# Down products of a mixture's experts in three passes of split operands, and transposes of the powers one piece earlier

## The chip, the cores and the metric

One core of one Trainium2 chip runs the whole kernel. The metric is the device time of one execution in microseconds (us), as the median of several runs; lower is better.

## What is computed

One decoder layer over 512 tokens of width 1024, in float32. First a token mixer (two recurrent branches, gates, an output projection, layer norm), then a mixture of 64 experts with top-8 routing, one shared expert and a gated embedding, and a second layer norm. The change lies in the experts, and for a small part at the very start. Of the reference:

```python
def routed_moe(x, ...):
    ...
    y = jnp.einsum('tf,fd->td', jax.nn.silu(xt @ ws_gate) * (xt @ ws_up), ws_down)
    for c in range(N_EXPERTS // EXPERT_CHUNK):
        sl = slice(c * EXPERT_CHUNK, (c + 1) * EXPERT_CHUNK)
        g = jnp.einsum('td,edf->tef', xt, w_gate[sl])
        u = jnp.einsum('td,edf->tef', xt, w_up[sl])
        hdn = jax.nn.silu(g) * u * combine[:, sl, None]
        y = y + jnp.einsum('tef,efd->td', hdn, w_down[sl])
```

Each expert has a gate and an up matrix of 1024x256 and a down matrix of 256x1024, 1 MB each. `combine` holds the routing weights, zero for all but eight experts of a token, so an expert sees 64 tokens on average (512 times 8 over 64); the kernel gathers them into 96 slots (`SL`). At the start, the mixer's input projection for the S5 branch is computed by `u_proj`, and the powers of the S5 transition are made on VectorE and turned by TensorE.

## The kernel before

The kernel is written engine by engine: one block each for SyncE (all large loads and stores), GpSimd, TensorE, ScalarE and VectorE. The order on each engine is the order of its block, and engines meet only in semaphores (`S["..."]`), each an ever growing count.

**Split operands.** A product of two float32 operands is made in one of two ways. A plain `mm` takes float32 operands as they are. `mm3` takes each operand as a high part (type fp32r, made by a ScalarE copy) and a low part (operand minus high part, made by a subtraction on VectorE or GpSimd), and adds three products: high by high, high by low, low by high (the profile's lines L701, L702, L703). Before, the experts' gate and up products are `mm3` products, and the down products (L1059) are plain.

**The experts' stage**, from about 840 us on, is a pipeline over 64 experts. Weights go through four buffers (`gate_up0..3`, `down0..3`), high parts of gate and up through two. For expert e (written `4 i + u` in the loops), one period of each engine is:

- TensorE (`expert`, from L1070 on): gate and up products of e (`gate_up`, 8 blocks of 3 products of 512 columns), eight transposes of the tokens of e+1 (`x_turn`), down products of e-1 (`down`, 2 halves by 2 blocks), two transposes of the hidden values of e (`hid_turn`).
- ScalarE: `gate_up_high(e+1)` (four copies of 128x1024), the silu of e, `rows_high(e+1)` (two copies, 128x384), `y_kept(e-1)` (first half of the down products' result from the bank to `yb`).
- VectorE: `gate_up_low(e+1)` (four subtractions of 128x1024, L1335), the product of silu, up value and routing weight (L1341), `rows_low(e+1)`, `y_kept(e-1)` (second half, L1834), and the copy of the turned hidden values from the bank, 128x192 (L1848).
- GpSimd: `gather(e+4)` (index copy L636, indirect DMA of token rows L639), then `add_expert(e-1)`: it waits for both halves of `y_kept(e-1)` and for the landing of the addition before (`rows_added`), copies an index column (L648), and issues the indirect DMA that adds up to 96 rows to `acc_dram` (L651). Additions are never in flight two at a time. `yb` has two buffers, so `y_kept(e)` waits for the landing of the addition of e-2.
- SyncE: `load_in(e+4)` once the gate and up products of e are done, `load_down(e+4)` once the down products of e are done.

Each engine's queue is in order: an instruction behind a waiting one waits too.

**The start.** `u_proj(0)` to `u_proj(7)` are eight pieces of the S5 projection (16 matmul records each, L735). Between the sixth, `u_proj(5)`, and the seventh, TensorE waits for `powers_ready` (VectorE has made the powers) and turns the powers (21 transposes, L708). VectorE waits for these (`powers_put`), copies them (L1456), works through a chain of element-wise instructions, and then makes the low parts of the transposed input (`x_low`), on which the first split products, `x_proj(0, 0)`, wait. `x_proj` also waits until ScalarE has copied all eight pieces of the projection (`u_kept`).

## Time and profile before

| | |
|---|---|
| median of 3 runs | 1528.13 us (1526.51 to 1529.31) |
| the profiled execution | 1527.41 us, span 1525.6 us |
| mean granted TensorE clock | 0.964 of full speed |
| TensorE busy | 92% of the span |
| HBM read, written | 297.35 MB, 34.65 MB |

The span runs from the first to the last instruction of the profiled execution; some 2 us of its time lie outside. A row of the timeline gives start and duration of an instruction, or of a run of equal ones (`x4`), and in brackets how long the engine had been idle before and what released it. DVE is VectorE, ACT ScalarE, POOL GpSimd, PE TensorE, SP SyncE. The durations of neighbours overlap a little, so for the rate at which instructions follow one another the starts are what counts.

### The profile page before, as it was taken

The page shows a single profiled execution, that of the slowest core. Times are in us where ns is not written, and L with a number is a line of the kernel's source. Part 1 is how long each engine was busy: PE and PEld are TensorE (multiplying, and loading weights), DVE is VectorE, ACT ScalarE, POOL GpSimd, SP SyncE. Part 2 cuts the span into 40 slices and gives each one's busy share as a digit, 9 for nine tenths or more (in the row PEclk, how much of TensorE's full clock was granted, in tenths as well). Part 3 has the DMA queues.
Part 4 walks back from the last instruction along what each step waited for, and adds up shares of the span by engine and source line. Part 5 has one row for each costly group of instructions (what it writes and reads, how often), then busy time and mean ns, then how long its engine had stood idle before and what let it go on. Part 6 is the DMA issues. An engine that isn't in the chain of part 4 may idle for free.

```text
span 1525.6 us, 18528 instructions
## 1 busy us (share of the span) xinstructions
PE 1408.9 (92%) x6293; PEld 931.9 (61%) x6293; DVE 867.1 (57%) x1240; ACT 608.1 (40%) x850; POOL 464.6 (30%) x415
## 2 busy tenths in 40 slices
PE   7979898998999999999957799999999999999990
PEld 4456777675788888555423466666666666666650
DVE  4598778785500100344712667766677667666655
ACT  3114654537422222010001555555555555555540
POOL 1012535333544443000261233222222222223322
PEclk8999999999899999999978899999999999999996
DMA  8035343434233334730045699999999999999953
GB/s 245 0 110 79 76 71 73 80 64 103 62 96 98 90 103 165 300 138 1 1 168 211 225 355 362 355 366 359 366 359 357 363 371 367 362 365 357 365 173 124
DMA packets 141491, 315.97 MB, mean 207 GB/s; under 512 B 18898, under 2 KB 100514, under 8 KB 116160
## 3 DMA queue, kind: packets, MB, share of 16 engines
q1 hardware_dynamic: 125984, 281.50, 53.3%
q0 software_dynamic: 15456, 33.79, 9.4%
q8 instruction: 33, 0.54, 0.1%
q14 instruction: 18, 0.15, 0.0%
HBM read 297.35 MB, written 34.65 MB: 218 GB/s over the span
## 4 chain that ended last, share of the span: by engine, by line
PE 75%; DVE 6%; DMA 6%; issue 4%; DVEq 2%; another core or an unknown queue 2%; POOL 2%; ACT 1%; POOLq 1%; SPq 0%; ACTq 0%
PE bank L701 14%; PE bank L703 14%; PE bank L702 14%; PE bank L1059 13%; PE bank L708 5%; PE bank L933 4%; PE bank L919 4%; PE bank L735 3%; DMA gate_up<-moe_w_up_in 3%; DVE arena L1335 3%; DVEq L1332 2%; DMA acc_dram<-arena 2%; PE bank L834 1%; POOLq L589 1%
## 5 line engine op out<-in xcount | busy, mean ns | idle before, releaser
L1335 DVE TENSOR_TENSOR gate_up_low<-gate_up,gate_up_high 128x1024 fp32r<-128x1024 f32 x256 | 296.5, 1220 | 98.4 <-ACT gate_up_high L1116 97.6
L1116 ACT ACTIVATE arena<-bank 96x512 f32<-96x512 f32 (+5 forms) x248 | 131.6, 554 | 413.2 <-PE bank L1059 138.4
L1116 ACT ACTIVATE gate_up_high<-gate_up 128x1024 fp32r<-128x1024 f32 x256 | 249.5, 1047 | 58.3 <-DMA gate_up<-moe_w_up_in 42.8
L1059 PE MATMUL bank<-down,arena 128*96 128x512 f32 x512 | 230.4, 592 | 1.0 <-DVE arena L1848 1.0
L1335 DVE TENSOR_TENSOR arena<-arena 128x512 f32<-128x512 f32 (+10 forms) x286 | 205.9, 752 | 18.9 <-ACT arena L1116 4.7
L701 PE MATMUL bank<-gate_up_high,rows_high 128*96 128x512 f32 x512 | 207.1, 404 | 5.4 <-DVE rows_low L1335 5.4
L703 PE MATMUL bank<-gate_up_high,rows_low 128*96 128x512 f32 x512 | 203.6, 398 | 0.0
L702 PE MATMUL bank<-gate_up_low,rows_high 128*96 128x512 f32 x512 | 202.0, 394 | 0.0
L708 PEld LDWEIGHTS bank<-arena 96*128 96x128 f32 (+4 forms) x1001 | 128.1, 186 | 66.4 <-issue 48.7
L554 POOL TENSOR_TENSOR wb_low<-arena,wb_high 128x1024 fp32r<-128x1024 f32 (+1 forms) x40 | 110.0, 2753 | 147.4 <-ACT wb_high L1116 147.4
L708 PE MATMUL bank<-arena 96*128 96x96 f32 (+4 forms) x1001 | 127.8, 267 | 18.6 <-DVE arena L1341 9.4
L1059 PEld LDWEIGHTS bank<-down,arena 128*96 128x96 f32 x512 | 80.3, 167 | 103.5 <-issue 103.4
L648 POOL COPY arena<-arena 96x1 int32 (+1 forms) x64 | 16.1, 252 | 348.7 <-DMA acc_dram<-arena 330.0
L554 POOL TENSOR_TENSOR wa_low<-arena,wa_high 128x1024 fp32r<-128x1024 f32 x24 | 61.4, 2573 | 186.5 <-ACT wa_high L1116 186.5
L1341 DVE SCALAR_TENSOR_TENSOR arena<-bank,arena 128x511 f32<-128x511 f32 (+3 forms) x44 | 32.2, 747 | 141.9 <-PE bank L703 139.6
L651 POOL DMA_INDIRECT acc_dram<-arena x64 | 94.8, 1481 | 58.5 <-POOL arena L648 52.4
L701 PEld LDWEIGHTS bank<-gate_up_high,rows_high 128*96 128x96 f32 x512 | 84.9, 166 | 38.1 <-issue 5.7
L703 PEld LDWEIGHTS bank<-gate_up_high,rows_low 128*96 128x96 f32 x512 | 82.9, 162 | 36.9
L1116 ACT ACTIVATE wb_high<-arena 128x1024 fp32r<-128x1024 f32 (+1 forms) x40 | 45.8, 1144 | 149.2 <-DMA arena<-w_glu_in 81.3
L702 PEld LDWEIGHTS bank<-gate_up_low,rows_high 128*96 128x96 f32 x512 | 83.6, 163 | 32.1
L1834 DVE COPY arena<-bank 96x512 f32<-96x512 f32 x64 | 44.0, 687 | 100.4 <-PE bank L1059 79.1
L1116 ACT ACTIVATE arena<-arena 128x512 f32<-128x512 f32 (+5 forms) x54 | 31.6, 609 | 167.4 <-DVE arena L1641 86.6
(150 smaller groups left out, 2161.8 us busy)
## 6 DMA issues: line engine op xcount, KB each, us to landing
gate_up<-moe_w_gate_in SPq DMA_DIRECT2D x64, 1024.0 KB
gate_up<-moe_w_up_in SPq DMA_DIRECT2D x64, 1024.0 KB
down<-moe_w_down_in SPq DMA_DIRECT2D x64, 1024.0 KB
arena<-w_in_in SPq DMA_DIRECT2D x40, 512.0 KB, 4.0
arena<-w_glu_in SPq DMA_DIRECT2D x16, 512.0 KB, 3.9
arena<-w_lru_out_in SPq DMA_DIRECT2D x8, 768.0 KB, 4.9
arena<-x_in SPq DMA_DIRECT2D x8, 512.0 KB, 5.2
arena<-w_in_in SPq DMA_DIRECT2D x2, 2048.0 KB, 11.7
```

The lines of the kernel that those rows point to most:

```text
L554: nc.gpsimd.tensor_tensor(lo, w, hi.bitcast(f32), ALU.subtract).then_inc(S["w_split"], 1)
L651: nc.gpsimd.indirect_dma_start(out=acc_dram, out_offset=bass.IndirectOffsetOnAxis(ap=idxcol[:, 4:5].bitcast(u32), axis=0), in_=yb[buf], in ...
L701: mm(dst, w_hi, v_hi, start=start, stop=False)
L702: mm(dst, w_hi, v_lo, start=False, stop=False)
L703: return mm(dst, w_lo, v_hi, start=False, stop=stop)
L708: return nc.tensor.transpose(dst, src, ident[0:n, 0:n])
L735: last = mm(banks[(5 + n) % 8][:, :], xT[:, k, t * P:(t + 1) * P], wu[:, k, hf * 512:(hf + 1) * 512], start=(k == 0), stop=(k == KD - 1))
L919: last = mm(banks[n % 4][:, :], merged[:, k, t * P:(t + 1) * P], wout[:, k, hf * 512:(hf + 1) * 512], start=(k == 0), stop=(k == KD - 1))
L933: last = mm(banks[hf][:, :], x1T[:, k, t * P:(t + 1) * P], pleg[:, k, hf * 512:(hf + 1) * 512], start=(k == 0), stop=(k == KD - 1))
L1059: last = mm(banks[5 + hf][0:SL, :], heT[u % 2][:, k], dn[u % 4][:, k, hs], start=(k == 0), stop=(k == 1))
L1116: return nc.scalar.activation(out_, in_, func, **kw)
L1335: return V_.tensor_tensor(out_, a, b_, op)
```

## The change

Of the experts: the down products become `mm3` products, 12 matmuls of fp32r in place of 4 of float32. For that each half of the down matrix, 128x1024, gets a high part on ScalarE (`down_high`, two copies, two new buffers) and a low part, written over the raw weights: the first half on VectorE, the second on GpSimd (`down_low`, behind `add_expert` in the same turn). The turned hidden values get a high part on ScalarE (`hid_high`) and a low part on VectorE, in place of VectorE's copy. The down products wait for both low parts. At the start: the powers' transposes stand behind the fifth piece of the projection instead of the sixth. (The names of semaphores in the branch for overflowing experts are merged too, which changes no order.)

```diff
@@ -258,7 +258,10 @@
         gu_lo = [part(f"gate_up_low{n}", o, 2 * KD, F) for n, o in enumerate(gu_at)]
-        heT = [at(b1 + 10240 + 512 * n, 2 * SL).rearrange("p (k s) -> p k s", k=2) for n in range(2)]
+        heT_hi = [part(f"hidden_high{n}", b1 + 10240 + 512 * n, 2, SL) for n in range(2)]
+        heT_lo = [part(f"hidden_low{n}", b1 + 10432 + 512 * n, 2, SL) for n in range(2)]
+        dn_hi = [part(f"down_high{n}", o, 2, D) for n, o in enumerate((b1 + 8192, sg_off))]
+        dn_lo = [part(f"down_low{n}", o, 2, D) for n, o in enumerate(dn_at)]
...
@@ -665,18 +669,26 @@
+            def down_low(i, u):
+                pool.wait_ge(S["dn_e_high"], 8 * i + 2 * u + 2)
+                nc.gpsimd.tensor_tensor(dn_lo[u % 4][:, 1], dn[u % 4][:, 1], dn_hi[u % 2][:, 1].bitcast(f32),
+                                        ALU.subtract).then_inc(S["dn_e_low1"], 1)
+
             for u in range(4):
                 pool.wait_ge(S["xT_e_put"], u + 1)
                 gather(4 + u, u, 4 + u)
                 if u:
                     add_expert(0, u - 1)
+                down_low(0, u)
             with pool.Fori(1, E // 4 - 1) as i:
                 for u in range(4):
                     pool.wait_ge(S["xT_e_put"], 4 * i + (u + 1))
                     gather(4 * i + (4 + u), u, 4 * i + (4 + u))
                     add_expert(i, u - 1)
+                    down_low(i, u)
             for u in range(E - 4, E):
                 add_expert(0, u - 1)
+                down_low(0, u)
             add_expert(0, E - 1)
...
@@ -743,7 +755,7 @@
-            for n in range(1, TT + 2):
+            for n in range(1, TT + 1):
                 u_proj(n)
             pe.wait_ge(S["powers_ready"], 1)
             pe.wait_ge(S["u_kept"], 2)
@@ -754,7 +766,7 @@
             last.then_inc(S["powers_put"], 1)
-            for n in range(TT + 2, 2 * TT):
+            for n in range(TT + 1, 2 * TT):
                 u_proj(n)
...
@@ -1049,14 +1061,16 @@
             def down(i, u):
-                pe.wait_ge(s_wdn[u % 4], 16 * i + 16 * (u // 4 + 1))
+                pe.wait_ge(S["dn_e_low0"], 4 * i + u + 1)
+                pe.wait_ge(S["dn_e_low1"], 4 * i + u + 1)
                 pe.wait_ge(S["hT_e_kept"], 4 * i + u + 1)
                 wait(pe, S["y_e_act"], 4 * i + u)
                 wait(pe, S["y_e_dve"], 4 * i + u)
                 for hf in range(2):
                     hs = slice(hf * 512, (hf + 1) * 512)
                     for k in range(2):
-                        last = mm(banks[5 + hf][0:SL, :], heT[u % 2][:, k], dn[u % 4][:, k, hs], start=(k == 0), stop=(k == 1))
+                        last = mm3(banks[5 + hf][0:SL, :], heT_hi[u % 2][:, k], heT_lo[u % 2][:, k],
+                                   dn_hi[u % 2][:, k, hs], dn_lo[u % 4][:, k, hs], k == 0, k == 1)
                 last.then_inc(S["y_e_put"], 1)
...
@@ -1281,6 +1295,16 @@
+            def down_high(i, u):
+                act.wait_ge(s_wdn[u % 4], 16 * i + 16 * (u // 4 + 1))
+                wait(act, S["y_e_put"], 4 * i + u - 1)
+                for k in range(2):
+                    f(dn_hi[u % 2][:, k], dn[u % 4][:, k], ACT.Copy).then_inc(S["dn_e_high"], 1)
+
+            def hid_high(i, u):
+                act.wait_ge(S["hT_e_put"], 4 * i + u + 1)
+                f(heT_hi[u % 2], banks[4][:, 0:2 * SL].rearrange("p (k x) -> p k x", k=2), ACT.Copy).then_inc(S["hT_e_high"], 1)
+
@@ -1294,8 +1318,10 @@
                 if more:
                     rows_high(i, u + 1)
+                down_high(i, u)
                 if not isinstance(i, int) or u >= 1:
                     y_kept(i, u - 1)
+                hid_high(i, u)
...
@@ -1841,11 +1867,14 @@
                 if more:
                     rows_low(i, u + 1)
+                dve.wait_ge(S["dn_e_high"], 8 * i + 2 * u + 1)
+                tt(dn_lo[u % 4][:, 0], dn[u % 4][:, 0], dn_hi[u % 2][:, 0].bitcast(f32), ALU.subtract).then_inc(S["dn_e_low0"], 1)
                 if not isinstance(i, int) or u >= 1:
                     y_kept(i, u - 1)
-                dve.wait_ge(S["hT_e_put"], 4 * i + u + 1)
+                dve.wait_ge(S["hT_e_high"], 4 * i + u + 1)
                 wait(dve, S["y_e_put"], 4 * i + u - 1)
-                V_.tensor_copy(heT[u % 2], banks[4][:, 0:2 * SL].rearrange("p (k x) -> p k x", k=2)).then_inc(S["hT_e_kept"], 1)
+                tt(heT_lo[u % 2], banks[4][:, 0:2 * SL].rearrange("p (k x) -> p k x", k=2), heT_hi[u % 2].bitcast(f32),
+                   ALU.subtract).then_inc(S["hT_e_kept"], 1)
```

Three places in the order of the instructions. First TensorE, at the start of the program; the rows are the projection's pieces (`128x512`) and the powers' transposes (`128x32 x21`). Before:

```order
L735 MATMUL bank<-arena 128x512 x8
L708 MATMUL bank<-arena 128x32 x64
L735 MATMUL bank<-arena 128x512 x40
L708 MATMUL bank<-arena 128x32 x21
L735 MATMUL bank<-arena 128x512 x16
```

And now:

```order
L747 MATMUL bank<-arena 128x512 x8
L720 MATMUL bank<-arena 128x32 x64
L747 MATMUL bank<-arena 128x512 x32
L720 MATMUL bank<-arena 128x32 x21
L747 MATMUL bank<-arena 128x512 x24
```

The 21 transposes moved ahead by one piece of eight products. Second VectorE, two experts' turns of the experts' stage. Before:

```order
L1335 TENSOR_TENSOR gate_up_low_133<-gate_up_121,gate_up_high_129 128x1024 x4
L1341 SCALAR_TENSOR_TENSOR arena<-arena,bank 96x256
L1335 TENSOR_TENSOR rows_low<-bank,rows_high 128x384 x2
L1834 COPY arena<-bank 96x512
L1848 COPY arena<-bank 128x192
```

And now:

```order
L1361 TENSOR_TENSOR gate_up_low_133<-gate_up_121,gate_up_high_129 128x1024 x4
L1367 SCALAR_TENSOR_TENSOR arena<-arena,bank 96x256
L1361 TENSOR_TENSOR rows_low<-bank,rows_high 128x384 x2
L1361 TENSOR_TENSOR down_low_142<-down_124,down_high_140 128x1024
L1860 COPY arena<-bank 96x512
L1361 TENSOR_TENSOR hidden_low_138<-bank,hidden_high_136 128x192
```

One subtraction of 128x1024 is new, and it stands ahead of the copy of the result; the copy of 128x192 became a subtraction. Third GpSimd, one turn inside the loop. Before:

```order
L636 COPY arena<-arena 96x1
L637 REGISTER_ALU
L639 DMA arena<-x_dram,arena 96x1024
L331 REGISTER_ALU
L648 ISA
L648 COPY arena<-arena 96x1
L651 DMA acc_dram<-arena 512x1024
```

And now:

```order
L640 COPY arena<-arena 96x1
L641 REGISTER_ALU
L643 DMA arena<-x_dram,arena 96x1024
L335 REGISTER_ALU
L652 ISA
L652 COPY arena<-arena 96x1
L655 DMA acc_dram<-arena 512x1024
L673 REGISTER_ALU
L674 TENSOR_TENSOR down_low_142<-down_124,down_high_140 128x1024
```

The subtraction of 128x1024 stands behind the index copy and the addition of the expert before, with both of which it shares a queue.

## Rows read from the trace of the kernel before

**Rows 1.** Page, part 1: busy us (share of the span), instructions

```profile
PE 1408.9 (92%) x6293; PEld 931.9 (61%) x6293; DVE 867.1 (57%) x1240; ACT 608.1 (40%) x850; POOL 464.6 (30%) x415
```

**Rows 2.** Windows (columns in its first line), experts' stage and first products

```profile
core 0: us, PE busy (x) PEld busy (x) DVE busy (x) ACT busy (x) POOL busy (x), PEclk, DMA share, GB/s
...
1200.00:1300.00 100.00, 100.00 (x419) 62.56 (x418) 68.17 (x91) 55.22 (x80) 28.40 (x40) 1.00 1.02 369
...
93.10:96.20 3.10, 3.10 (x7) 2.45 (x8) 3.10 (x6) 0.00 (x0) 0.00 (x0) 0.51 0.72 167
```

**Rows 3.** Timeline, one expert's period, all engines: start us, us, what

```profile
1201.09 3.60 PE L1059 MATMUL bank<-down,arena 128*96 128x512 f32 x8
...
1202.30 0.47 DVE L1341 SCALAR_TENSOR_TENSOR arena<-arena,bank 96x256 f32<-96x256 f32 x1
...
1202.69 1.01 DVE L1335 TENSOR_TENSOR rows_low<-bank,rows_high 128x384 fp32r<-128x384 f32 x2
...
1204.67 0.45 PE L701 MATMUL bank<-gate_up_high,rows_high 128*96 128x512 f32 x1
...
1204.80 0.69 DVE L1834 COPY arena<-bank 96x512 f32<-96x512 f32 x1 [1.09 <-issue]
...
1205.40 0.34 DVE L1848 COPY arena<-bank 128x192 f32<-128x192 f32 x1
...
1206.68 3.90 ACT L1116 ACTIVATE gate_up_high<-gate_up 128x1024 fp32r<-128x1024 f32 x4 [1.30 <-DMA gate_up<-moe_w_up_in]
...
1207.78 4.63 DVE L1335 TENSOR_TENSOR gate_up_low<-gate_up,gate_up_high 128x1024 fp32r<-128x1024 f32 x4 [2.03 <-ACT gate_up_high L1116]
...
1210.29 1.02 PE L708 MATMUL bank<-arena 96*128 96x96 f32 x8
...
1211.15 3.60 PE L1059 MATMUL bank<-down,arena 128*96 128x512 f32 x8
```

**Rows 4.** Timeline of GpSimd, two periods and the last two additions

```profile
1203.47 1.47 POOL L651 DMA_INDIRECT acc_dram<-arena  x1 [0.89 <-POOL arena L648]
1204.46 0.67 POOL L636 COPY arena<-arena 96x1 int32 x1
...
1212.43 0.18 POOL L648 COPY arena<-arena 96x1 int32 x1 [5.44 <-DMA acc_dram<-arena]
...
1488.93 1.44 POOL L651 DMA_INDIRECT acc_dram<-arena  x1 [0.86 <-POOL arena L648]
...
1494.60 1.44 POOL L651 DMA_INDIRECT acc_dram<-arena  x1 [0.92 <-POOL arena L648]
```

**Rows 5.** Timeline, first stage: TensorE and VectorE

```profile
71.19 14.00 PE L735 MATMUL bank<-arena 128*128 128x512 f32 x32
93.11 0.76 PE L701 MATMUL bank<-x_high,wa_high 128*128 128x512 f32 x1 [7.91 <-DVE x_low L1335]
...
47.07 8.59 DVE L1335 TENSOR_TENSOR arena<-arena 32x128 f32<-32x128 f32 x18
71.30 0.69 DVE L1456 COPY arena<-bank 128x512 f32<-128x512 f32 x1 [15.64 <-PE bank L708]
...
92.27 4.91 DVE L1335 TENSOR_TENSOR x_low<-arena,x_high 128x512 fp32r<-128x512 f32 x8 [0.19 <-issue]
```

**Rows 6.** Timeline: VectorE beside GpSimd at three places, and one source line's durations

```profile
234.65 2.72 DVE L1335 TENSOR_TENSOR arena<-arena 128x512 f32<-128x512 f32 x1
...
238.75 0.69 DVE L1335 TENSOR_TENSOR arena<-arena 128x512 f32<-128x512 f32 x1
...
231.66 5.17 POOL L554 TENSOR_TENSOR wa_low<-arena,wa_high 128x1024 fp32r<-128x1024 f32 x2
...
391.54 7.30 DVE L1335 TENSOR_TENSOR lru_low<-arena,lru_high 128x512 fp32r<-128x512 f32 x12
...
393.72 9.74 POOL L554 TENSOR_TENSOR wb_low<-arena,wb_high 128x1024 fp32r<-128x1024 f32 x2 [3.86 <-ACT wb_high L1116]
...
L554 POOL TENSOR_TENSOR wb_low<-arena,wb_high x40: 2357/2398/7380, 352.7 to 600.7; 128x1024 fp32r<-128x1024 f32 x32, 128x1536 fp32r<-128x1536 f32 x8
```

More of the change, by code:

```diff
@@ L315, in decoder_layer @@
             xT_e_put xT_e_high xT_e_low g_e_put silu_e hid_e hT_e_put hT_e_kept y_e_put y_e_act y_e_dve
+             hT_e_high dn_e_high dn_e_low0 dn_e_low1
              gu_e_high gu_e_low
-             o_w o_xT_put o_xT_kept o_g_put o_silu o_hid o_hT_put o_hT_kept o_y_put o_y_kept
+             o_w         o_y_kept o_put o_act o_dve
             over_done out_ready out_stored""".split()
@@ L1093, in _ @@
                                 last = tp(banks[h][:, k * SL:(k + 1) * SL], xv[:, 4 * h + k, :], SL)
-                        last.then_inc(S["o_xT_put"], 1)
-                        pe.wait_ge(S["o_xT_kept"], i + 1)
+                        last.then_inc(S["o_put"], 1)
+                        pe.wait_ge(S["o_dve"], 3 * i + 1)
                         pe.wait_ge(S["o_w"], 48 * i + 48)
@@ L1098, in _ @@
                             last = mm(banks[2][0:SL, :], xgT[:, k, :], gu[0][:, k, :, :], start=(k == 0), stop=(k == KD - 1))
-                        last.then_inc(S["o_g_put"], 1)
-                        pe.wait_ge(S["o_hid"], i + 1)
+                        last.then_inc(S["o_put"], 1)
+                        pe.wait_ge(S["o_dve"], 3 * i + 2)
                         hv = hid_e[0].rearrange("p (d k) -> p k d", k=2)
@@ L1103, in _ @@
                             last = tp(banks[4][:, k * SL:(k + 1) * SL], hv[:, k, :], SL)
-                        last.then_inc(S["o_hT_put"], 1)
-                        pe.wait_ge(S["o_hT_kept"], i + 1)
+                        last.then_inc(S["o_put"], 1)
+                        pe.wait_ge(S["o_dve"], 3 * i + 3)
                         for hf in range(2):
@@ L1109, in _ @@
                                           start=(k == 0), stop=(k == 1))
-                        last.then_inc(S["o_y_put"], 1)
+                        last.then_inc(S["o_put"], 1)
                     pe.nop()
@@ L1317, in _ @@
                     with act.If(i < n_over):
-                        act.wait_ge(S["o_xT_put"], i + 1)
-                        f(xgT[:, 0:4, :], banks[0][:, 0:4 * SL].rearrange("p (k x) -> p k x", k=4), ACT.Copy).then_inc(S["o_xT_act"], 1)
-                        act.wait_ge(S["o_g_put"], i + 1)
-                        f(hid_e[0], banks[2][0:SL, 0:F], ACT.Silu).then_inc(S["o_silu"], 1)
+                        act.wait_ge(S["o_put"], 4 * i + 1)
+                        f(xgT[:, 0:4, :], banks[0][:, 0:4 * SL].rearrange("p (k x) -> p k x", k=4), ACT.Copy).then_inc(S["o_act"], 1)
+                        act.wait_ge(S["o_put"], 4 * i + 2)
+                        f(hid_e[0], banks[2][0:SL, 0:F], ACT.Silu).then_inc(S["o_act"], 1)
                     act.nop()
@@ L1866, in _ @@
                     with dve.If(i < n_over):
-                        dve.wait_ge(S["o_xT_act"], i + 1)
-                        V_.tensor_copy(xgT[:, 4:8, :], banks[1][:, 0:4 * SL].rearrange("p (k x) -> p k x", k=4)).then_inc(S["o_xT_kept"], 1)
-                        dve.wait_ge(S["o_silu"], i + 1)
+                        dve.wait_ge(S["o_act"], 2 * i + 1)
+                        V_.tensor_copy(xgT[:, 4:8, :], banks[1][:, 0:4 * SL].rearrange("p (k x) -> p k x", k=4)).then_inc(S["o_dve"], 1)
+                        dve.wait_ge(S["o_act"], 2 * i + 2)
                         stt(hid_e[0], hid_e[0], gateT[:, bass.ds(i + E, 1)], banks[2][0:SL, F:2 * F],
-                            ALU.mult, ALU.mult).then_inc(S["o_hid"], 1)
-                        dve.wait_ge(S["o_hT_put"], i + 1)
-                        V_.tensor_copy(ohT[:, :, 0:SL], banks[4][:, 0:2 * SL].rearrange("p (k x) -> p k x", k=2)).then_inc(S["o_hT_kept"], 1)
-                        dve.wait_ge(S["o_y_put"], i + 1)
+                            ALU.mult, ALU.mult).then_inc(S["o_dve"], 1)
+                        dve.wait_ge(S["o_put"], 4 * i + 3)
+                        V_.tensor_copy(ohT[:, :, 0:SL], banks[4][:, 0:2 * SL].rearrange("p (k x) -> p k x", k=2)).then_inc(S["o_dve"], 1)
+                        dve.wait_ge(S["o_put"], 4 * i + 4)
                         V_.tensor_copy(yb[0][:, 0:512], banks[5][0:SL, :])
```

2 lines of the change are left out of this document (1 added, 1 removed).

## The prediction

> **What bounds the kernel now.** The page's first part comes first: TensorE is busy for 92% of the span, VectorE for 57%, GpSimd for 30% [rows 1]. These shares are averages over unlike stages, so the windows come next. In the experts' stage TensorE has no idle time at all, at the full granted clock, while the DMA share is 1.02 and 369 GB/s flow; VectorE is busy for 68 of 100 us there, ScalarE for 55 [rows 2]. The timeline of one expert gives the period: the down products start at 1201.09 and again at 1211.15, **10.06 us** later [rows 3]. So TensorE sets the pace, with DMA just under it. A third loop is as tight: GpSimd issues the addition of an expert's rows at 1203.47, and its landing lets the next index copy start at 1212.43, 8.96 us later; from the index copy to the issue it is another 0.89 idle plus 0.18, so 8.96 + 1.07 = 10.03 us at least from addition to addition [rows 4]. Three things stand within a per cent of each other: TensorE's order, DMA, and the additions' loop. That is the first thing to see: taking time from one alone gives little.
>
> At the start, TensorE's first split product waits 7.91 us for VectorE's x_low [rows 5]. VectorE in turn was idle for 15.64 us before 71.30, until TensorE's transposes [rows 5], although its last instruction on the powers ended at 47.07 + 8.59 = 55.66.
>
> **The change, term by term.** I count against the profiled execution (1527.41 us, 0.7 below the median).
>
> *The start.* One piece of the projection takes half of 14.00 us, 7.0, or by starts some 6.9 [rows 5]. The transposes move ahead of one such piece; the powers are ready at 55.66, before TensorE gets there (about 63), so nothing new waits for them. VectorE's chain begins 6.9 us earlier, and x_low, which began at 92.27, begins at about 85.4. TensorE ends the projection when it did, at 71.19 + 14.00 = 85.2, and ScalarE's last copy of it follows within a microsecond, so the first split product moves from 93.11 to about 86.2: **-6.9 us**. It may get a little more: the seven products after that idle time ran at a granted clock of 0.51, 3.10 us for seven [rows 2], where 24 gate and up products take 5.62 us at the full clock [rows 3], so some 1.4 us less for seven; the idle time will be about 1 us in place of 8. All later work follows TensorE here. I take -7.5; the bounds are 0 (another wait takes its place) and -8.4.
>
> *TensorE in the experts' stage.* Down products took 3.5 us (3.60 less the overlap) [rows 3]. In three passes they are 12 products, at 5.62 over 24, 0.234 each: 2.8 us. That is 0.64 us per expert, 41 us over 64, if TensorE stayed the pace-maker.
>
> *ScalarE* gets two copies of 128x1024 (3.90 over 4, so 0.97 each [rows 3]) and one of 128x192, together 2.3 us on 5.5: 7.8 of 10.06. It fits.
>
> *VectorE*, by starts in one period [rows 3]: four low parts of gate and up 4.63, the hidden values 0.39, rows_low 1.01, copy of the result 0.60, copy of 128x192 0.34: 6.97 us. The change adds a fifth 128x1024 subtraction, 4.63 / 4 = 1.16, and a subtraction for the last copy (128x384 in 0.50, so between 0.34 and 0.50; I take 0.40). Sum 8.2 us. Alone that fits too.
>
> *GpSimd* gets one 128x1024 subtraction, median 2.40 us in the earlier stages [rows 6]. Here lies the cost. Rows show that such a GpSimd instruction and a VectorE instruction with two operands in SBUF don't run together. At 234.65 a 128x512 two-operand instruction of VectorE took 2.72 us in place of 0.69, while GpSimd ran two of its own from 231.66 to 236.83 [rows 6]. And from 393.72 two of GpSimd's took 9.74 us in place of 4.8, because VectorE was in a run of twelve from 391.54 to 398.84 [rows 6]. In the Trainium skill, "SBUF — State Buffer", section "Who interferes with whom", VectorE with two SBUF inputs and a GpSimd instruction that reads SBUF exclude each other for whole instructions, whichever issued first going first; the rows agree on the exclusion.
>
> Can the 2.4 us fall where VectorE reads banks or rests? Take D as the start of the down products of expert e. They end at D + 2.8, the result is copied by VectorE until about D + 3.8, the index copy and issue take 1.07: the addition of e starts no sooner than D + 4.9, and the next GpSimd instruction 0.99 later (1203.47 to 1204.46 [rows 4]), at D + 5.9. VectorE's run of four gate and up low parts starts when ScalarE is through with the hidden values and its first copy, 2.8 + 0.4 for the transposes, 0.4, and 1.1: about D + 4.8, and lasts until D + 9.5. GpSimd's subtraction always becomes ready inside this run. So it takes VectorE's time: 8.2 + 2.4 = 10.6 us, and the two index copies, which read SBUF too, add 0.1 to 0.2: **10.75 us per expert**, VectorE without a pause. TensorE then waits about 1.3 us per expert, first of all for GpSimd's low part. That is 0.69 us more than now on 62 periods from the first down products to those of expert 62: **+43 us**.
>
> *The end.* The last down products wait for GpSimd's low part, which stands behind the addition of expert 62. From down products to down products there: 2.8, copy 1.0, index and issue 1.1, 0.99, 2.4, so 8.3 us, against some 5.7 between the last two additions now (1488.93 to 1494.60 [rows 4]): **+2.6 us**.
>
> Sum: -7.5 + 43 + 2.6 = +38 us. Against the median of 1528.1 that is **1566 us**. For the likeliest case alone, with a period between 10.5 and 11.1 us, the bounds are 62 x 0.44 = 27 and 62 x 1.04 = 64, so with the start between -8.4 and 0 its own range is 1549 to 1595.
>
> **The rivals.**
>
> *GpSimd is kept out of the whole run.* If its subtraction must wait until VectorE's four are done, as at 393.72 it waited for some eight [rows 6], it starts at D + 9.5 and ends at D + 12: TensorE's next down products start then, a period of 12.0 us. 62 x 1.94 = 120, plus 2.6, less 7.5: 1643 us. It may also be kept out for one or two of the four, or only in some periods: 11.1 to 12 us, 1590 to 1643. The skill's rule, by which an instruction that issued first goes first, would let GpSimd in at the next boundary, and gives the 1566. The row at 393.72 speaks for the rival; for the rule speaks the same view at 231.66, where two of GpSimd's ran unbroken. Chance 0.25 for all periods above 11.1.
>
> *The subtraction finds room, and the stage keeps its pace.* If GpSimd and VectorE don't exclude each other in this place, the period can't fall to TensorE's 9.4 us, because the DMA share is 1.02 already and the additions' loop needs 10.03 [rows 2, 4]. The stage keeps its 10.06 or gains 0.03 per expert, 2 us; the end costs 2.6, and what is left is the start: **faster**, 1518 to 1523 us. This is the case on the other side. It decides itself at the point where VectorE's work plus what GpSimd blocks stays under 10.06, so if less than 1.8 of the 2.4 us blocks. For it speaks that VectorE has 3 us free now; against it, the phase argument above. Chance 0.12.
>
> *Something between*, a period of 10.1 to 10.5 us: 1523 to 1549. Chance 0.10.
>
> *TensorE's saving arrives in full*: 1528.1 - 7.5 - 41 = 1480 us. It needs 3 MB of weights in 9.4 us besides gathered and added rows, where all sixteen DMA engines are already busy. The skill's summary table in the same page puts a load from HBM at about 358 GB/s; the windows of this stage show 369. Chance 0.02.
>
> **How the numbers follow.** Likeliest 0.51 (1549 to 1595), kept out 0.25 (1590 to 1645), between 0.10, room 0.12, full saving 0.02. The range of 8 in 10 goes from 1521 to 1625: it leaves out about half of the room case, the full saving, and a third to a half of the kept-out case. A measurement here can tell about 0.2%, 3 us, from no change. Faster than that: room, full saving and the low edge of the between case, 0.14. Within it, part of the between case, 0.02. Slower: 0.84.
>
> **What would show it right or wrong.** In the profile after: the first split product near 86 us and x_low no longer its releaser by 8 us; the start of the down products every 10.75 us; VectorE busy for over 80 of 100 us in the middle of the stage, with single 128x1024 subtractions of 3.5 us among those of 1.2; GpSimd's subtraction at 2.4 us or more, and TensorE idle before the down products, released by GpSimd; a DMA share under 1. If the GpSimd subtraction took 2.4 us and none of VectorE's grew, the port argument is wrong. If the period is about 12 with GpSimd's subtraction at 5 to 6 us, the first rival holds. If the DMA share stays at 1.02 and TensorE waits for weights or additions at a period near 10.06, the second does.

## The result, and the profile after

| | before | after |
|---|---|---|
| median of 4 runs | 1527.32 us (1525.73 to 1529.31) | **1735.94 us** (1733.45 to 1738.00) |
| ratio, 95% interval | 1 | 1.1358 [1.1337, 1.1379] |
| profiled execution, span | 1527.41, 1525.6 us | 1738.00, 1736.2 us |
| mean granted TensorE clock | 0.964 | 0.909 |
| down products, first and last start | 859.04, 1488.10 | 853.71, 1698.12 |
| mean period of an expert | 9.99 us | 13.40 us |

The change costs 13.6%, some 209 us. The forecast was 1566 us, with a range up to 1625: the direction was right, the size was not. The last two rows of the table say where the time lies: 63 periods that are 3.42 us longer make +215, the experts' first down products come 5.3 us earlier, together +210 against the 210.6 between the two spans.

Part 1 of the page, after, which answers to [rows 1]:

```profile
PE 1463.8 (84%) x6549; PEld 1023.2 (59%) x6549; DVE 1096.1 (63%) x1304; ACT 745.2 (43%) x1042; POOL 810.5 (47%) x479
```

Busy times in three windows, after: 100 us of the stage, as in [rows 2], and the down products of two neighbouring experts. Columns as in [rows 2]: length, busy time of PE, PEld, DVE, ACT and POOL with their instructions, granted clock, DMA share, GB/s.

```profile
1200.00:1300.00 100.00, 80.02 (x330) 56.54 (x330) 76.34 (x70) 54.92 (x80) 64.41 (x39) 0.86 0.77 264
1205.20:1210.40 5.20, 5.20 (x12) 3.36 (x13) 1.00 (x1) 0.00 (x0) 2.04 (x2) 0.50 0.21 54
1217.60:1220.40 2.80, 2.80 (x12) 2.02 (x13) 2.80 (x4) 2.71 (x4) 1.93 (x2) 1.00 1.01 336
```

Nobody is full any more: TensorE is busy for 80 of 100 us, VectorE for 76, and DMA fell from a share of 1.02 to 0.77. When every engine has idle time and the stage is slower, a chain from engine to engine sets the period. The experiments below test that. The second and third rows show something else: the same twelve products take 5.20 us at a granted clock of 0.50, half of full speed, and 2.80 at 1.00.

GpSimd's timeline over two experts, after (start, duration, engine, line; in brackets the idle time before and its releaser). L652 is the index copy of the addition, L655 the issue of the addition's DMA, L674 the new subtraction; L640 and L643 belong to the gather.

```profile
1195.93 4.45 POOL L652 COPY arena<-arena 96x1 int32 x1 [2.57 <-DVE arena L1860]
1201.26 1.46 POOL L655 DMA_INDIRECT acc_dram<-arena  x1 [0.89 <-PE bank L720]
1202.27 2.83 POOL L674 TENSOR_TENSOR down_low<-down,down_high 128x1024 fp32r<-128x1024 f32 x1
1204.56 1.66 POOL L640 COPY arena<-arena 96x1 int32 x1
...
1211.81 0.18 POOL L652 COPY arena<-arena 96x1 int32 x1 [3.70 <-DVE arena L1860]
1212.87 2.20 POOL L655 DMA_INDIRECT acc_dram<-arena  x1 [0.89 <-POOL arena L652]
1214.61 2.89 POOL L674 TENSOR_TENSOR down_low<-down,down_high 128x1024 fp32r<-128x1024 f32 x1
```

VectorE's timeline over the same two experts, after:

```profile
1193.72 1.21 DVE L1361 TENSOR_TENSOR down_low<-down,down_high 128x1024 fp32r<-128x1024 f32 x1
1194.85 0.68 DVE L1860 COPY arena<-bank 96x512 f32<-96x512 f32 x1
1195.45 0.34 DVE L1361 TENSOR_TENSOR hidden_low<-bank,hidden_high 128x192 fp32r<-128x192 f32 x1
1195.72 4.62 DVE L1361 TENSOR_TENSOR gate_up_low<-gate_up,gate_up_high 128x1024 fp32r<-128x1024 f32 x4
...
1202.41 3.79 DVE L1361 TENSOR_TENSOR down_low<-down,down_high 128x1024 fp32r<-128x1024 f32 x1 [0.31 <-ACT down_high L1130]
1210.72 0.69 DVE L1860 COPY arena<-bank 96x512 f32<-96x512 f32 x1 [4.52 <-PE bank L715]
1211.55 0.36 DVE L1361 TENSOR_TENSOR hidden_low<-bank,hidden_high 128x192 fp32r<-128x192 f32 x1
1212.50 7.23 DVE L1361 TENSOR_TENSOR gate_up_low<-gate_up,gate_up_high 128x1024 fp32r<-128x1024 f32 x4 [0.59 <-ACT gate_up_high L1130]
```

TensorE's timeline, the first down product of three experts in a row, after:

```profile
1190.35 0.44 PE L713 MATMUL bank<-down_high,hidden_high 128*96 128x512 f32 x1
...
1205.20 0.71 PE L713 MATMUL bank<-down_high,hidden_high 128*96 128x512 f32 x1 [4.68 <-issue]
...
1217.60 0.45 PE L713 MATMUL bank<-down_high,hidden_high 128*96 128x512 f32 x1
```

Read the three together. The subtraction stands in GpSimd's order behind the addition of the expert before. So there is a closed loop: down products, VectorE's copy of their result (L1860), index copy, issue, subtraction, next down products. **Long turn** (ends with the products at 1205.20): the index copy takes 4.45 us, from 1195.93 to 1200.38, where it takes 0.18 in the other turn. It begins 0.21 us after VectorE's run of four, which has no idle time before or within it (1.16 us each), and ends with it. TensorE is idle for 4.68 us, and its next products run at half clock. (The bracket names no releaser, but GpSimd's subtraction ended at 1205.10, the last of what these products wait for.) **Short turn** (ends at 1217.60): because those products ended late, VectorE is early this time and waits 0.59 us for ScalarE's first copy before its run. The index copy takes 0.18, from 1211.81, and is over before the run starts at 1212.50. The subtraction, from 1214.61, gets in among the four, ahead of VectorE's third, which makes VectorE's run 7.23 in place of 4.62. The two turns alternate through the stage: the down products come after 14.9 and 12.4 us, in most pairs.

The third instruction of that run did not have to wait for ScalarE, whose copies for the two runs are these:

```profile
1194.15 3.90 ACT L1130 ACTIVATE gate_up_high<-gate_up 128x1024 fp32r<-128x1024 f32 x4
...
1211.41 3.89 ACT L1130 ACTIVATE gate_up_high<-gate_up 128x1024 fp32r<-128x1024 f32 x4
```

Three of the later four are done by about 1214.4, and VectorE's second subtraction ends near 1214.9. So its third was ready half a us before, and GpSimd went first all the same. What the two turns differ in is how VectorE's run begins: without any idle time in the long turn, after 0.59 us of it in the short one.

### The profile page after: what moved, and what is told of

Read it like the earlier page. It is cut to its first block, busy times and chain, and to the rows that moved or that the text cites. A ratio compares the mean times of both kernels' runs of the same rounds, so it can differ in the third digit from the quotient of the medians.

```text
span 1736.2 us, 19534 instructions
## 1 busy us (share of the span) xinstructions
PE 1463.8 (84%) x6549; PEld 1023.2 (59%) x6549; DVE 1096.1 (63%) x1304; ACT 745.2 (43%) x1042; POOL 810.5 (47%) x479
## 4 chain that ended last, share of the span: by engine, by line
PE 63%; issue 14%; DVE 12%; DVEq 2%; DMA 2%; POOL 2%; ACT 2%; another core or an unknown queue 2%; POOLq 1%; SPq 0%; ACTq 0%
PE bank L713 16%; PE bank L715 15%; PE bank L714 15%; DVE arena L1361 4%; PE bank L945 3%; PE bank L931 3%; DVE gate_up_low L1361 3%; PE bank L720 3%; PE bank L747 2%; DVEq L1358 2%; DVE rows_low L1361 2%; DMA acc_dram<-arena 1%; PE bank L965 1%; DVE arena L1367 1%
## 5 line engine op out<-in xcount | busy, mean ns | idle before, releaser
L1361 DVE TENSOR_TENSOR gate_up_low<-gate_up,gate_up_high 128x1024 fp32r<-128x1024 f32 x256 | 377.8, 1534 | 31.3 <-ACT gate_up_high L1130 31.3
L713 PE MATMUL bank<-down_high,hidden_high 128*96 128x512 f32 x256 | 133.2, 520 | 157.7 <-issue 151.4
L652 POOL COPY arena<-arena 96x1 int32 (+1 forms) x64 | 139.1, 2174 | 211.1 <-DVE arena L1860 208.1
L674 POOL TENSOR_TENSOR down_low<-down,down_high 128x1024 fp32r<-128x1024 f32 x64 | 183.3, 2864 | 4.8 <-ACT down_high L1130 4.8
L713 PEld LDWEIGHTS bank<-down_high,hidden_high 128*96 128x96 f32 x256 | 54.0, 211 | 187.1 <-issue 168.2
L1361 DVE TENSOR_TENSOR down_low<-down,down_high 128x1024 fp32r<-128x1024 f32 x64 | 152.3, 2380 | 9.9 <-ACT down_high L1130 9.9
L655 POOL DMA_INDIRECT acc_dram<-arena x64 | 118.5, 1851 | 58.5 <-POOL arena L652 31.0
L1860 DVE COPY arena<-bank 96x512 f32<-96x512 f32 x64 | 43.6, 681 | 146.4 <-PE bank L715 146.4
L1130 ACT ACTIVATE down_high<-down 128x1024 fp32r<-128x1024 f32 x128 | 128.4, 1059 | 0.0
L714 PE MATMUL bank<-down_low,hidden_high 128*96 128x512 f32 x256 | 128.1, 500 | 0.0
L715 PE MATMUL bank<-down_high,hidden_low 128*96 128x512 f32 x256 | 127.4, 497 | 0.0
```

Source lines behind the costliest of these rows:

```text
L652: nc.gpsimd.tensor_copy(idxcol[:, 4:5].bitcast(i32), idxT[:, bass.ds(e, 1)].bitcast(i32)).then_inc(S["sc_col"], 1)
L655: nc.gpsimd.indirect_dma_start(out=acc_dram, out_offset=bass.IndirectOffsetOnAxis(ap=idxcol[:, 4:5].bitcast(u32), axis=0), in_=yb[buf], in ...
L674: nc.gpsimd.tensor_tensor(dn_lo[u % 4][:, 1], dn[u % 4][:, 1], dn_hi[u % 2][:, 1].bitcast(f32), ALU.subtract).then_inc(S["dn_e_low1"], 1)
L713: mm(dst, w_hi, v_hi, start=start, stop=False)
L714: mm(dst, w_hi, v_lo, start=False, stop=False)
L715: return mm(dst, w_lo, v_hi, start=False, stop=stop)
```

## Experiments

Each kernel is compared with the kernel before, run beside it. There are three groups: e1, e2, e3, e5; then e4, e6, e7, e9; then e8, e10, e11. The kernel before took 1528.8, 1515.6 and 1527.7 us in them, so ratios are what compares. The changed kernel was not run again in these groups; its ratio of 1.1358 stands for it. Mean periods are taken over all 63 periods between down products, where the kernel before has 9.99 us.

### The two parts of the change apart, and the subtraction moved

**e1_front_alone**: the kernel before with only the start's part.

```diff
-            for n in range(1, TT + 2):
+            for n in range(1, TT + 1):
...
-            for n in range(TT + 2, 2 * TT):
+            for n in range(TT + 1, 2 * TT):
```

> The kernel before with the powers' transposes behind the fifth piece, nothing else. In the trace of the changed kernel the first split product begins at 88.53 us in place of 93.11. If the start gives what the forecast said, this run is 4.5 to 8 us faster than before. If another wait takes its place later on (a load, the S5 store), it is within 1 us of before.

Measured: 1518.13 us, ratio 0.9920 [0.9903, 0.9938]; the same kernel again beside the last group (**e11_front_again**) 1518.18, 0.9941 [0.9928, 0.9953].

> The first run's kernel again, beside the two others on one chip, for a comparison of the versions: ratio 0.990 to 0.995, by its profiled span 7.8 us less than before.

TensorE and VectorE at the start, e1_front_alone, and the window behind the idle time, which answers to the second of [rows 2]:

```profile
87.41 0.47 PE L701 MATMUL bank<-x_high,wa_high 128*128 128x512 f32 x1 [1.05 <-DVE x_low L1335]
```

```profile
86.57 4.91 DVE L1335 TENSOR_TENSOR x_low<-arena,x_high 128x512 fp32r<-128x512 f32 x8 [0.19 <-PE bank L735]
```

```profile
87.40:90.50 3.10, 3.09 (x14) 2.55 (x15) 3.10 (x6) 0.00 (x0) 0.00 (x0) 1.00 0.83 330
```

The first split product starts at 87.41 in place of 93.11, with an idle time of 1.05 in place of 7.91; the down products of the first expert start at 852.43 in place of 859.04, and the span is 7.8 us shorter (9.6 in e11). In 3.10 us behind this idle time fourteen products run at the full clock, where seven ran at 0.51 behind 7.91 us of it.

**e2_experts_alone**: the changed kernel with the start's order of before (the edit of e1 taken back).

> The changed kernel with the powers' transposes behind the sixth piece again. If the two parts of the change don't touch each other, it takes the changed kernel's time plus what the first run saves: 1740 to 1744 us. If the expert stage's rhythm depends on when it starts, it differs from that by more than 5 us.

Measured: 1744.40, ratio 1.1412 [1.1391, 1.1433]. The two parts add up (1744.4 less 10.7 is 1733.7, of 1735.9): the whole loss is in the experts' part.

**e3_low_on_vector**: the changed kernel, with the second half's low part on VectorE; GpSimd gets no subtraction.

```diff
 tt(dn_lo[u % 4][:, 0], dn[u % 4][:, 0], dn_hi[u % 2][:, 0].bitcast(f32), ALU.subtract).then_inc(S["dn_e_low0"], 1)
+dve.wait_ge(S["dn_e_high"], 8 * i + 2 * u + 2)
+tt(dn_lo[u % 4][:, 1], dn[u % 4][:, 1], dn_hi[u % 2][:, 1].bitcast(f32), ALU.subtract).then_inc(S["dn_e_low1"], 1)
...
-                    down_low(i, u)
```

> The changed kernel with both low parts of the down matrix on VectorE and none on GpSimd. Theory 1 (the loss comes from GpSimd's subtraction in the path of the down products: it stands behind an index copy that VectorE's run of four keeps out, and blocks VectorE in turn): VectorE then has 9.4 us per expert and nothing waits for GpSimd, the period is 10.1 to 10.6 us and the time 1522 to 1560 us. Theory 2 (three passes with their extra waits, or the load of ScalarE and VectorE, are too much by themselves): over 1600 us, with TensorE waiting for VectorE's low parts.

Measured: 1524.36, ratio 0.9983 [0.9961, 1.0006]. The window of the stage, e3_low_on_vector:

```profile
1200.00:1300.00 100.00, 95.75 (x454) 68.34 (x453) 90.41 (x108) 74.58 (x109) 35.33 (x40) 1.00 1.02 363
```

Some 210 us (1.1358 less 0.9983, of 1528.8) are gone with one instruction per expert on another engine. VectorE carries some 9.2 us of work per expert (0.904 of 10.2). The first eight periods are 9.4 us, which is TensorE's new order, and then the mean is 10.2 (up to the last full period) with the DMA share at 1.02, as before; over all periods it is 10.02. So the saving of 0.64 us per expert is there at first and then goes. It isn't quite free either: beside e1, in the same group, e3 is 6 us slower, so it gives back more than half of what the start saves. The waits of this kernel in the stage (us in total, times, longest) say who is waited for:

```profile
POOL arena L652 <- DMA acc_dram<-arena: 259.5, 53, 6.8
ACT arena L1122 <- DMA acc_dram<-arena: 120.7, 52, 3.2
```

The landings of the additions are waited for in nearly every period, with the DMA engines full. That full transfers take the saving is argued from the share and these waits; no run makes the transfers lighter.

**e5_low_before_addition**: the changed kernel, with the subtraction still on GpSimd, but ahead of the addition.

```diff
-                    add_expert(i, u - 1)
                     down_low(i, u)
+                    add_expert(i, u - 1)
```

> The changed kernel with GpSimd's subtraction ahead of the addition of the expert before, behind the gathering. The work and its exclusion with VectorE stay, only its place in the queue changes. If the queue place is what costs (the subtraction waits for the result of the down products before it and for the index copy): 1550 to 1620 us, a period of 10.6 to 11.5, and no idle time of TensorE of over 2 us. If the exclusion itself costs, wherever the subtraction stands: over 1680 us.

Measured: 1552.53, ratio 1.0161 [1.0140, 1.0183]. GpSimd's timeline of one expert, VectorE's run beside it, the index copy over all experts (ns, min/median/max), and the window of the stage, e5_low_before_addition:

```profile
1202.47 2.49 POOL L674 TENSOR_TENSOR down_low<-down,down_high 128x1024 fp32r<-128x1024 f32 x1 [0.61 <-ACT down_high L1130]
1206.27 0.96 POOL L652 COPY arena<-arena 96x1 int32 x1 [1.30 <-DMA acc_dram<-arena]
```

```profile
1204.24 5.21 DVE L1361 TENSOR_TENSOR gate_up_low<-gate_up,gate_up_high 128x1024 fp32r<-128x1024 f32 x4 [0.59 <-ACT gate_up_high L1130]
```

```profile
L652 POOL COPY arena<-arena x64: 178/1172/1226, 854.5 to 1517.1; 96x1 int32 x56, 96x1 int32<-96x1 int32 x8
```

```profile
1200.00:1300.00 100.00, 92.71 (x436) 67.27 (x435) 86.17 (x97) 74.18 (x107) 70.40 (x47) 0.97 0.97 347
```

The subtraction is back at 2.49 us, most of it lies ahead of VectorE's run (from 1204.24), and 183 of the 210 us are gone: the order on GpSimd, which closes the loop, costs the time, and not the 2.5 us themselves. The mean period is 10.52. Most periods are 9.42, but thirteen take 12.6 to 15.3, and TensorE is idle for up to 4.3 us there, where the expectation had no idle time of over 2. In each of the thirteen one GpSimd instruction is kept out until VectorE's run has ended: nine times the issue of the gather (5.36 to 7.48 us), three times the subtraction (up to 6.72), once the gather's index copy (7.02). All thirteen of VectorE's runs there begin without idle time. The index copy of the addition, on the other hand, falls into a run in nearly every period and never takes more than 1.23 us, at most about one instruction of VectorE's: these runs began after idle time (as the one at 1204.24), or behind an instruction that GpSimd had already delayed.

### Which instruction is held out, and when

**e4_index_early**: the changed kernel, with the index copy of the addition made earlier, right behind the gather, into a column of its own for even and odd experts. Only the issue stays between the result and the subtraction.

```diff
+def add_col(buf, e, n):
+    wait(pool, S["rows_added"], 16 * (n - 1))
+    pool.sem_inc(S["col_seen"], 1)
+    nc.gpsimd.tensor_copy(idxcol[:, 4 + buf:5 + buf].bitcast(i32), idxT[:, bass.ds(e, 1)].bitcast(i32)).then_inc(S["sc_col"], 1)
...
 def add_expert(i, u):
+    add_col(u % 2, 4 * i + u, 4 * i + u)
     pool.wait_ge(S["y_e_act"]
```

> The changed kernel with the index copy of an addition made right behind the gathering, before GpSimd waits for the result of the down products (two index columns in turn). In the changed kernel every second index copy took 4.4 us in place of 0.18, held out by VectorE's run of four, and every second period was 14.9 us. Theory 1 (that index copy is what makes the long periods): the copy takes under 1.7 us everywhere and the time falls by over 60 us, to 1600 to 1675. Rival (the subtraction behind the addition now meets the same run of VectorE and is kept out in its place): the subtraction's duration grows to 5 to 7 us and the time stays over 1700 us.

Measured: 1677.76, ratio 1.1062 [1.1025, 1.1100]. GpSimd's timeline, e4_index_early (here L659 is the issue, L679 the subtraction):

```profile
1204.32 1.47 POOL L659 DMA_INDIRECT acc_dram<-arena  x1 [3.00 <-issue]
1205.33 2.90 POOL L679 TENSOR_TENSOR down_low<-down,down_high 128x1024 fp32r<-128x1024 f32 x1
...
1211.35 0.28 POOL L652 COPY arena<-arena 96x1 int32 x1
1215.70 5.09 POOL L659 DMA_INDIRECT acc_dram<-arena  x1 [4.07 <-issue]
1220.34 2.84 POOL L679 TENSOR_TENSOR down_low<-down,down_high 128x1024 fp32r<-128x1024 f32 x1
```

VectorE's two runs beside them, e4_index_early:

```profile
1204.42 7.17 DVE L1367 TENSOR_TENSOR gate_up_low<-gate_up,gate_up_high 128x1024 fp32r<-128x1024 f32 x4 [0.59 <-ACT gate_up_high L1136]
...
1214.83 4.62 DVE L1367 TENSOR_TENSOR gate_up_low<-gate_up,gate_up_high 128x1024 fp32r<-128x1024 f32 x4
```

The copy is short in nearly all turns now (median 0.28), and the issue takes its place: 5.09 us beside the run that begins without idle time, 1.47 where it comes 0.1 us ahead of the run that begins after 0.59 us of it; there the subtraction gets in behind VectorE's first instruction. So it is not the copy: whatever GpSimd has next is held out to the end of a run that began without a pause. The mean period is 12.7, still alternating. Neither expectation came true as a whole: the copy was short and 45 us went, not 60, and of the rival only its kind came true, with the issue in place of the subtraction.

**e6_gaps**: the changed kernel, with a drain of VectorE behind each low part of gate and up, so that no two of the four follow one another at once.

```diff
 tt(gu_lo[u % 4][:, ks], gu_raw[u % 4][:, ks], gu_hi[u % 2][:, ks].bitcast(f32), ALU.subtract).then_inc(S["gu_e_low"], 1)
+d()
```

> The changed kernel with a VectorE drain behind each of the four gate and up subtractions, so that VectorE is never ready with the next one at once. Theory (GpSimd gets the shared read access only where VectorE's next instruction is not yet ready to start; a run whose inputs are all ready keeps it out): no index copy takes over 1.7 us, GpSimd's subtraction goes ahead inside the run, the long periods vanish, and the time falls to 1600 to 1690 us although VectorE has more to do. Rival (a run keeps GpSimd out whether or not there are gaps): index copies of 4.4 us and more stay, and the time is 1736 us or more.

Measured: 1619.65, ratio 1.0695 [1.0655, 1.0735]: slower instructions on VectorE, and the whole kernel 6% faster than the changed one (1.0695 over 1.1358). The index copy over all experts (ns, min/median/max), the changed kernel and then e6_gaps:

```profile
L652 POOL COPY arena<-arena x64: 177/182/4682, 857.8 to 1704.1; 96x1 int32 x56, 96x1 int32<-96x1 int32 x8
```

```profile
L652 POOL COPY arena<-arena x64: 177/180/1274, 840.4 to 1578.0; 96x1 int32 x56, 96x1 int32<-96x1 int32 x8
```

VectorE's run where all is ready, e6_gaps:

```profile
1207.70 1.21 DVE L1361 TENSOR_TENSOR gate_up_low<-gate_up,gate_up_high 128x1024 fp32r<-128x1024 f32 x1
1209.08 1.23 DVE L1361 TENSOR_TENSOR gate_up_low<-gate_up,gate_up_high 128x1024 fp32r<-128x1024 f32 x1 [0.17 <-issue]
1210.47 1.23 DVE L1361 TENSOR_TENSOR gate_up_low<-gate_up,gate_up_high 128x1024 fp32r<-128x1024 f32 x1 [0.16 <-issue]
1211.86 3.27 DVE L1361 TENSOR_TENSOR gate_up_low<-gate_up,gate_up_high 128x1024 fp32r<-128x1024 f32 x1 [0.16 <-issue]
```

With 0.16 us between them GpSimd gets in behind the first instruction that ends: its longest copy is 1.27 us, one of VectorE's, and its subtraction holds VectorE's fourth (3.27). The loop is closed still, and the mean period is 11.7; the run began without idle time, so it is the drains that let GpSimd in. The long periods are 12.4 us, where they were 14.9. The expectation's theory, that GpSimd gets in only where VectorE's next instruction isn't ready, goes further than this run shows, and the short turn of the changed kernel is against it.

**e7_filler**: the changed kernel, with four float32 products of constant data into a free bank ahead of the down products' wait; their result isn't used.

```diff
 def down(i, u):
+    for _ in range(4):
+        mm(banks[7][0:SL, :], lnp[:, 2, 0:SL], lnp[:, 3, 0:512], start=True, stop=True)
     pe.wait_ge(S["dn_e_low0"], 4 * i + u + 1)
...
+pe.wait_ge(S["lnp_loaded"], 16 * 6)
```

> The changed kernel with four float32 products of static data into the free bank, 3.4 us at full clock, ahead of TensorE's wait for the low parts of the down matrix. They compute nothing that is used. Theory (TensorE's down products in the long periods run at the lower clock because TensorE was idle for 4.7 us before): the idle time is filled, the twelve products take 2.8 us each time in place of 5.2 every second time, and the time is within 40 us of the changed kernel (the filler also costs in the short periods). Rival (the lower clock has nothing to do with the idle time): they still take 5.2 us every second time, and the time is over 1780 us.

Measured: 1682.79, ratio 1.1109 [1.1070, 1.1148]. The window of the stage, and the index copy over all experts, e7_filler:

```profile
1200.00:1300.00 100.00, 100.00 (x424) 64.39 (x423) 82.91 (x76) 61.32 (x88) 54.85 (x39) 1.00 0.82 287
```

```profile
L652 POOL COPY arena<-arena x64: 178/179/183, 842.3 to 1648.7; 96x1 int32 x56, 96x1 int32<-96x1 int32 x8
```

TensorE does 3.45 us of useless work per expert, and the kernel is 2% faster than the changed one (1.1109 over 1.1358). The alternation is gone: each period is 12.85 (but for the last two), VectorE's runs take 7.20 and begin after a wait for ScalarE, and no index copy is held out (183 ns at most): it is over before the run begins. But the filler also sets the period here: TensorE is busy for 100 of 100 us, 9.4 + 3.45 = 12.85. So this run shows that the clock stays up when TensorE is kept busy, and that the hold depends on the phase; it is no measure of what the clock alone costs. That measure is the window after, 5.20 against 2.80.

### Is there a better version?

**e8_vector_and_early** is e3 with the edit of e4; **e9_front_early** the kernel before with the edits of e1 and e4; **e10_low_first_index_early** is e5 with the index copy of e4, put ahead of the subtraction:

```diff
+                    add_col((u - 1) % 2, 4 * i + (u - 1), 4 * i + (u - 1))
                     down_low(i, u)
                     add_expert(i, u - 1)
```

> Both low parts of the down matrix on VectorE (as in the third run, ratio 0.998) and the index copies made early. If the additions' loop, with ScalarE and VectorE waiting for landings in nearly every period of the third run, is what kept that one from using TensorE's 9.4 us: ratio 0.985 to 0.993. If DMA alone keeps the pace at 10.1 us (its share was 1.02 there): ratio 0.993 to 1.000, no better than the front alone.

> The kernel before with the transposes moved (as in the first run, 1518 us) and the index copies of the additions made early. If the additions' loop (10.03 us and more per expert) bounds the experts' stage beside TensorE's 10.06, the loop falls to about 9 us and the stage ends up to 10 us sooner: 1508 to 1516 us. If TensorE's order and DMA bound it alone: 1515 to 1520.

> GpSimd's subtraction ahead of the addition (ratio 1.016 in that run, periods of 9.4 us broken by one of 14 to 16 us every fourth or fifth) and the index copy made early, ahead of the subtraction. If the broken periods come from an index copy or an issue that VectorE's run holds out, the early copy removes part of them: ratio 1.000 to 1.010. If they come from the subtraction itself, which took up to 6.7 us: 1.010 to 1.025.

| kernel | median, us | ratio, 95% interval | mean period, us |
|---|---|---|---|
| e11_front_again | 1518.18 | 0.9941 [0.9928, 0.9953] | 10.00 |
| e8_vector_and_early | 1517.89 | 0.9929 [0.9910, 0.9947] | 9.95 |
| e10_low_first_index_early | 1524.47 | 0.9978 [0.9967, 0.9988] | 10.07 |
| e9_front_early (second group) | 1507.47 | 0.9944 [0.9924, 0.9963] | 10.07 |

e8 has 9.4 in its first ten periods and 10.15 in the mean from there to the last full one, with a DMA share of 1.02: the saved TensorE time mostly doesn't come through. The earlier index copy seems to help e3 and e5: e8 is 0.5% under e3, and e10 1.8% under e5 and below both of its expectations, as far as ratios of different groups compare. In e10 most periods are 9.4, and eight take 12.8 to 14.2, in each of which a GpSimd instruction took 4.56 us or more. An earlier index copy gives nothing to e9, whose interval overlaps those of e1 and e11 (its expected times were for a kernel before of 1528 us; that one took 1515.6 beside it). No version beats the start's part alone by more than its interval.

## Why the prediction was wrong in size

**The start: right, somewhat small.** Forecast -7.5 (bounds 0 and -8.4), mechanism as told. In the profiles of e1 and after the first split product came 5.7 and 4.6 us earlier, not 6.9: in e1 x_low began at 86.57, not 85.4, and after's first stretch of the projection took 8.66 us in place of 6.99. By the end of the span it was 7.8 and 9.6 us in e1 and e11. The medians say 10.7 and 9.5 us. What the last microseconds are is open.

**ScalarE, VectorE and TensorE: right.** e3 shows it: with all low parts on VectorE the stage takes 631.5 us from its first to its last down products, 629.1 before, and TensorE's order is 9.4 us. Its 0.64 us don't arrive, with the DMA share at 1.02, as the rival of the full saving had it.

**GpSimd: the failed steps are three.**

1. *"The two index copies, which read SBUF too, add 0.1 to 0.2."* This is the largest. I priced them at their own length. By my own working the copy came at D + 3.8, a us ahead of VectorE's run at D + 4.8, and I let the result be copied at once, though VectorE's fifth subtraction stands ahead of that. In the long turn the copy came at D + 5.6, 0.2 us into a run that had begun at D + 5.4. It took 4.45 us in every second turn, with 0.18 in the other: 4.3 us per pair of experts. e4 shows that the next instruction takes over the wait if the copy is moved.
2. *"VectorE without a pause"* as what sets the period, 8.2 + 2.4. After, VectorE is busy for 76 of 100 us. What sets it is the closed loop. I had all its parts, even the sum, under *The end*: "2.8, copy 1.0, index and issue 1.1, 0.99, 2.4, so 8.3 us". I took that as the price of the last expert and not as a bound that holds for every period and stretches with each delay in it. The working below sums it as it ran. e5 opens the loop and gives back 183 of the 210 us.
3. *TensorE at full clock.* Forecast for the twelve products 2.8 us; after an idle time of 4.7 us they took 5.20, at 0.50: 2.4 us per pair of experts, inside the loop. I had used this effect at the start [rows 2] and not asked for it in the experts' stage. It follows from the first two steps: with the idle time as forecast, 1.3 us, it need not have come, as after 1.05 us in e1 the clock was full.

The loop, by the starts above and the products at 1190.35:

| from ... to | forecast | short turn (to 1217.60) | long turn (to 1205.20) |
|---|---|---|---|
| down products | 2.8 | 5.2 | 2.8 |
| their end to the index copy | 1.0 | 1.4 | 2.8 |
| index copy to the issue | 1.1 | 1.06 | 5.33 |
| issue to subtraction | 1.0 | 1.74 | 1.01 |
| subtraction to down products | 2.4 | 2.99 | 2.93 |
| sum | 8.3 | 12.4 | 14.9 |

The two turns take 27.3 us where twice the loop as I had summed it takes 16.6. Of the 10.7 between, the held copy is 4.3 and the half clock 2.4. VectorE's copy of the result comes late by 2.2 in all (in the long turn the fifth subtraction stands ahead of it, at 1193.72), the two subtractions, up to the products behind them, are 1.1 longer than their median of before, and the issue beside VectorE's run 0.7.

**The rivals.** *Kept out of the whole run*, at 0.25, was right in kind and wrong in two things: which instruction is kept out (the index copy or the issue, not the subtraction) and the fixed period of 12.0; the real mean is 13.4, with the late copy of the result and the clock on top. The row at 393.72 of [rows 6] was the one to trust, beside a run of twelve with no idle time before it, and not the one at 231.66. The Trainium skill, "SBUF — State Buffer", section "Who interferes with whom", has it that what issued first goes first. That fits where VectorE pauses between its instructions (e6), and index copies that wait for one instruction of VectorE's in e5. It doesn't fit the long turns: there GpSimd issued during VectorE's first instruction, before ScalarE had made the second one's operand (the copy at 1195.93, the operand near 1196.1), and ran after the fourth, 4.45 us in place of at most one instruction's 1.16. *Finds room* fell: the subtraction does block (3.79 for VectorE's of 1.21). Of the signs named, single VectorE subtractions of 3.8, GpSimd's at 2.8 and a DMA share under 1 came true; the period of 10.75, VectorE busy for over 80 of 100 us (76) and the first split product near 86 (88.53) didn't. Nor did the trace name GpSimd as TensorE's releaser, though its subtraction ended 0.1 us before the products.

**Open.** Why a run that begins without idle time keeps GpSimd out to its end, where one that begins after some lets it in at the next boundary, isn't shown. In the experts' stage of the changed kernel, e2, e4, e5 and e10, all instructions of GpSimd that were kept out to a run's end met a run of the first kind (30 each in the changed kernel, e2 and e4, 13 in e5, 8 in e10); e7 has no such run, and in e6 the drains break it. But only e6 and e7 change this by an edit, and e7 moves the index copy out of the run as well. Nor does a run show what brings the work of e5 into such a phase every few periods.

## What to carry to other kernels

Before putting a step into another engine's order, write down the loop that it closes, from the product back to itself, and sum it: that sum is a floor for every period, and each delay inside it counts in full. A small GpSimd instruction beside a run of VectorE instructions with two operands in SBUF is not priced at its own duration but, where that run follows VectorE's earlier work without idle time, at the length of the run. And where a forecast leaves TensorE idle as long as in a stretch of the trace after which its clock is half, the next products are priced at that clock.

## What the runs showed of the hardware that was not expected

- A GpSimd instruction that becomes ready within a run of VectorE's two-operand SBUF instructions waited for the end of the run where the run had begun without idle time (0.18 becomes 4.45 for a 96x1 copy). It got in at a boundary where the run had begun after idle time, though VectorE's next one was ready half a us before (the subtraction at 1214.61; index copies of at most 1.23 us in e5), or where drains leave 0.16 us between VectorE's instructions (at most 1.27).
- The issue of an indirect DMA on GpSimd is held the same way: 5.09 us against 1.47 (e4), 5.36 and more in e5.
- A system of such waits has two phases that alternate, 14.9 and 12.4 us, in a program that does the same for every expert; useless products that keep TensorE's clock up (e7) put all turns into the same phase, and made the kernel 2% faster.
